# A norm's column sums: the first third laid into the last product block, and two accumulations of squares put ahead of the seventh tile's addition

## What is computed

```python
def rms_norm(x, g):
    xf = x.astype(jnp.float32)
    y = xf * lax.rsqrt(jnp.mean(xf * xf, axis=-1, keepdims=True) + EPS)
    return (y * g.astype(jnp.float32)).astype(x.dtype)

x = x + g1 * jnp.einsum('blm,md->bld', mix, w_out[l])                 # mixer's output product
x = x + g2 * swiglu(modulate(rms_norm(x, norm2_g[l]), sh2, sc2),      # feed-forward
                    w_ffn_in[l], w_ffn_out[l])
```

## Time and profile before

| | |
|---|---|
| median of 3 executions | 2637.63 us |
| the three | 2633.22, 2637.63, 2647.82 us |
| profiled execution, its own time | 2635.52 us |
| its span in the profile | 2633.7 us |
| mean granted TensorE clock | 0.959 of full |
| TensorE matmul records, busy | 13049, 94% of the span |
| VectorE, ScalarE, GpSimd busy | 51%, 30%, 33% |
| matmul records of line 673 on `n_acc` | 72 in 7 norms |

### The profile page before, as it was taken

The page is one execution under the profiler, slowest core; times in us unless marked ns, Lnnn a source line. Parts: engine busy times, 40 slices in busy tenths (PEclk is TensorE's granted clock), DMA queues, the critical chain, the costliest instruction groups (busy, mean ns, idle before and its releaser), DMA issues.

```text
span 2633.7 us, 30775 instructions
## 1 busy us (share of the span) xinstructions
PE 2481.7 (94%) x13049; PEld 2029.7 (77%) x13049; DVE 1341.3 (51%) x1704; ACT 795.0 (30%) x1083; POOL 875.5 (33%) x613
## 2 busy tenths in 40 slices
PE   7999699999999999897999999989999989999998
PEld 4889578888888888696777778878887437788886
DVE  2997865645444434877566655564642223311113
ACT  2323661311111112335631222234433333322223
POOL 2000502233333333434034554534333002444442
PEclk9998899999999999998999999989999998999999
DMA  8233103224343342221044554521103001232331
GB/s 266 91 96 97 49 1 112 81 80 128 120 136 92 116 120 64 80 90 49 1 112 144 146 172 145 177 80 51 47 17 117 11 1 48 72 104 84 100 95 58
DMA packets 309225, 240.57 MB, mean 91 GB/s; under 512 B 10692, under 2 KB 304831, under 8 KB 309087
## 3 DMA queue, kind: packets, MB, share of 16 engines
q1 hardware_dynamic: 308674, 238.47, 29.9%
q10 hardware_dynamic: 414, 0.13, 0.0%
HBM read 232.29 MB, written 2.10 MB: 89 GB/s over the span
## 4 chain that ended last, share of the span: by engine, by line
PE 87%; DVE 8%; ACT 3%; issue 1%; DMA 1%; POOL 0%; SPq 0%; DVEq 0%; ACTq 0%
PE ps L2486 61%; PE ps L1148 5%; PE ps L2521 3%; PE ps L722 2%; PE ps L935 2%; DVE mod_w L2118 1%; PE ps L1168 1%; PE ps L673 1%; DVE mod_ctx L2118 1%; PE ps L2401 1%; DVE qk_lo L875 1%; PE ps L2438 1%; PE ps L1191 1%; PE ps L749 1%; ACT probs L979 1%
## 5 line engine op out<-in xcount | busy, mean ns | idle before, releaser
L1631 POOL TENSOR_TENSOR w_lo<-raw,w_hi 128x512 fp32r<-128x512 f32 x518 | 756.5, 1490 | 1576.6 <-ACT w_hi L1732 1576.6
L2486 PE MATMUL ps<-h_hi,w_hi 128*128 128x512 f32 x1994 | 650.3, 372 | 25.1 <-DVE h_lo L2082 21.0
L2486 PE MATMUL ps<-h_lo,w_hi 128*128 128x512 f32 x1994 | 640.5, 367 | 0.0
L2486 PE MATMUL ps<-h_hi,w_lo 128*128 128x512 f32 x1994 | 639.6, 367 | 0.0
L1732 ACT ACTIVATE w_hi<-raw 128x2048 fp32r<-128x2048 f32 (+2 forms) x155 | 264.9, 1709 | 595.3 <-PE ps L2486 368.5
L2486 PEld LDWEIGHTS ps<-h_hi,w_hi 128*128 128x128 f32 x1994 | 341.0, 191 | 94.0 <-issue 23.1
L2486 PEld LDWEIGHTS ps<-h_hi,w_lo 128*128 128x128 f32 x1994 | 340.3, 190 | 66.7
L2486 PEld LDWEIGHTS ps<-h_lo,w_hi 128*128 128x128 f32 x1994 | 341.0, 191 | 65.7 <-issue 0.2
L2009 ACT ACTIVATE xg<-ps 128x512 f32<-128x512 f32 (+1 forms) x66 | 44.2, 670 | 678.5 <-PE ps L2486 491.6
L2118 DVE SCALAR_TENSOR_TENSOR mod_w<-mod_w,cond 128x512 f32<-128x512 f32 x224 | 240.7, 1075 | 3.4
L2486 PE MATMUL ps<-hid_hi,w_hi 128*128 128x512 f32 x704 | 232.1, 370 | 0.0
(11 more groups left out here) (367 smaller groups left out, 3244.5 us busy)
## 6 DMA issues: line engine op xcount, KB each, us to landing
mod_w<-in_w_mod SPq DMA_DIRECT2D x72, 1024.0 KB, 9.4
raw<-in_w_ffn_in SPq DMA_DIRECT2D x88, 512.0 KB, 5.3
raw<-in_w_in SPq DMA_DIRECT2D x54, 512.0 KB, 5.1
raw<-in_w_ffn_out SPq DMA_DIRECT2D x48, 384.0 KB, 3.8
raw<-in_w_out SPq DMA_DIRECT2D x24, 512.0 KB, 4.7
raw<-in_w_gate SPq DMA_DIRECT2D x22, 512.0 KB, 4.0
raw<-in_w_up SPq DMA_DIRECT2D x22, 512.0 KB, 5.4
raw<-in_w_down SPq DMA_DIRECT2D x24, 384.0 KB, 3.9
```

Source lines behind the costliest of these rows:

```text
L1631: ins = pool.tensor_tensor(w_lo[:, s, at:end], raw[:, s, at:end], w_hi[:, s, at:end].bitcast(F32), ALU.subtract)
L2486: ins = pe.matmul(ps[0:m, at:at + tw], weight(part, k, cols), v[:, held[k] if held else k, t0:t0 + tw], start=(at_k == 0 and j == 0 and no ...
```

## The change

On VectorE, `add_block(ni, 2)` (the accumulation of the squares of tiles 4 and 5) is issued ahead of the wait on `gemm_tile` and of tile 6's addition to `x`, instead of behind that addition. On TensorE, the column sums of `n_acc` (the first of three sources) are issued in the last block of products, for its second output tile, behind contraction step `k_tiles - 2`, so that one step of three products still follows; the norm itself then begins with the second source. Norm 0 keeps all three sources where they were. The waits stay the same: PSUM's bank half 0 free, and five accumulations done; they are now met inside the product stream.

```diff
@@ -2136,6 +2136,7 @@
                 for t in range(2):
                     if ni and b == 3 and t == 0:
+                        add_block(ni, 2)
                         dve.wait_ge(gemm_tile, ni)
                     else:
                         dve.wait_ge(gemm_done, n + 1)
@@ -2146,7 +2147,6 @@
                     if ni and b == 3 and t == 0:
                         ins.then_inc(n_x, 1)
-                        add_block(ni, 2)
@@ -2410,17 +2410,21 @@
-            def norm(ni, next_block):
-                pe.wait_ge(psum_free[0], freed(next_block)) if next_block else None
+            def norm_sum(ni, next_block, i):
+
+                if i == 0:
+                    pe.wait_ge(psum_free[0], freed(next_block)) if next_block else None
+                    pe.wait_ge(n_added, NORM_ADDED * (ni + 1))
+                else:
+                    pe.wait_ge(n_sq, KD * ni + KD - 2 + i)
+                ins = token_columns(pe, 0, (n_acc[:, :], sq[:, 0, :], sq[:, 1, :])[i], norm_tokens(ni) // P, i == 0, i == 2)
+                if i == 2:
+                    ins.then_inc(n_ss, 1)
+
+            def norm(ni, next_block, first=0):
                 T = norm_tokens(ni)
-
-                for i, (src, needed) in enumerate(((n_acc[:, :], None), (sq[:, 0, :], KD - 1), (sq[:, 1, :], KD))):
...
-                ins.then_inc(n_ss, 1)
+                for i in range(first, 3):
+                    norm_sum(ni, next_block, i)
@@ -2503,6 +2507,8 @@
                             if among and (t, at_k) != (tiles - 1, k_tiles - 1):
                                 among(t, at_k)
+                            if ni and t == 1 and at_k == k_tiles - 2:
+                                norm_sum(ni, n + 1, 0)
@@ -2554,7 +2560,7 @@
-                norm(2 * l, base_in[l])
+                norm(2 * l, base_in[l], 1 if l else 0)
@@ -2751,7 +2757,7 @@
-                norm(2 * l + 1, base_ffn[l])
+                norm(2 * l + 1, base_ffn[l], 1)
@@ -2768,7 +2774,7 @@
-                norm(6, blocks_used)
+                norm(6, blocks_used, 1)
```

More of the change, by code:

```diff
@@ L2411, in first_mods @@
                         ins.then_inc(mod_cols, 1)
-            def norm(ni, next_block):
-                pe.wait_ge(psum_free[0], freed(next_block)) if next_block else None
-                T = norm_tokens(ni)
-                for i, (src, needed) in enumerate(((n_acc[:, :], None), (sq[:, 0, :], KD - 1), (sq[:, 1, :], KD))):
[L2418 to L2422, removed]
-                ins.then_inc(n_ss, 1)
+            def norm_sum(ni, next_block, i):
[8 more added lines that the diff above has]
+            def norm(ni, next_block, first=0):
+                T = norm_tokens(ni)
+                for i in range(first, 3):
+                    norm_sum(ni, next_block, i)
                 pe.wait_ge(psum_free[1], freed(next_block)) if next_block else None
```

## The result

| | kernel before | changed kernel |
|---|---|---|
| median of 20 executions each | 2637.57 us | 2647.16 us |
| lowest to highest | 2633.22 to 2647.82 | 2635.41 to 2651.30 |
| profiled execution, its span | 2633.7 us | 2633.6 us |
| granted clock in the span | 0.959 | 0.960 |

The account below looks back on a forecast made before the run. TensorE's product stream was taken to bound the kernel (87% of the chain). Boundary terms +1.11, +1.20, 0.88, 1.0, 0.88, 0.88 gave +5.95, say 6.0 us, from 2636.6 to 2642.6; range 2633 to 2652.

Parts of the forecast that it names:

- The price of a record: In the product stream: each small sum costs 0.11 us, so 1.32 for twelve and 0.88 for eight.
- ScalarE's branch ends last at four of the six boundaries: Between last product and root: TensorE's sums end last at only two of six boundaries, once by only 0.23 us.
- sums done over 1.5 us ahead of the root: Sign at the third, fifth and sixth boundary: root still directly behind ScalarE's weights or load, sums done long before.
- No wait on `n_acc`: Second and sixth boundary: TensorE meets no stall on the fifth accumulation, with 0.2 and 0.5 us to spare.
- the 0.12 to be won back: Second boundary: tile 7's addition no longer waits for the accumulations, giving back 0.12 us; net there +1.20.
- the fourth boundary, +1.93 for +1.0: Fourth boundary: a 1.9 us stall in mid-product replaces the 1.88 behind it; root at 1753.60 against 1752.64, net +1.0.
- Then 1.32 of sums and 0.88 of products: Fourth boundary, TensorE behind the mid-product stall: sums and remaining products take these times; last product ends at 1748.77.
- the rival in which waits spread to other boundaries: Mid-product waits also at second and sixth boundary, clock falling inside: 2642.6 + 3.8 + 6 = 2652.4; chance 0.09.
- the upper bound of 0.145 for a record: Product stream: a record costs at most the fourth boundary's tail rate, 5.23 / 36; 60 records then cost 8.7 us.
- The clock's phase behind the boundaries: Products after each boundary: a small shift changes their half-clock loss between 1.5 and 3.0 us; 2638.5 to 2647.7; chance 0.20.
- The rival that the change does nothing: Whole kernel: the order only looks different, 0 us, 2636.6; chance 0.16 shared with records costing nothing.
- the sums are swallowed: Records cost nothing in the stream and the fourth boundary's stall goes: -2.6 us, 2634.0; chance 0.16, shared with no difference.

Follow-up runs that it names:

- the accumulations alone: Kernel before with only `add_block(ni, 2)` moved ahead of the wait on `gemm_tile`, the sums left behind the last product; ratio 1.0004 (0.9992 to 1.0017).
- the even boundaries only: Changed kernel with `n_acc` sums inside the last block only at the second, fourth and sixth boundary; ratio 1.0016 against the kernel before.
- the sums alone: Changed kernel with the accumulations of tiles 4 and 5 put back behind tile 6's addition; ratio 1.0055 against the kernel before, 14.5 us slower.
- the sums four times: Changed kernel with the `n_acc` sums issued three times more in the same place, into unread PSUM columns; ratio 1.0177 against the kernel before, 46.7 us.
- the changed kernel with the root first: Changed kernel with ScalarE taking the root ahead of the early weights' high parts; ratio 1.0019 against the kernel before, +5.0 us.
- the root first: Kernel before with ScalarE taking the root ahead of the early weights' high parts, sums where they were; ratio 1.0002 (0.9991 to 1.0013).
- the root first and six accumulated: Kernel before, root ahead of the early weights' high parts, tile 6's square also accumulated into `n_acc` at odd boundaries; ratio 0.9997 (0.9987 to 1.0008).

## Why the prediction was right

**What held.** The sign, the size (+6.0 forecast, +6.6 measured) and the way to it. The price of a record from layer 1's head sums, 0.11, gave 0.88 and 1.32; the third and sixth boundary came out at 0.88 and 0.90. The reading that ScalarE's branch ends last at four of the six boundaries held, and with it that nothing comes back there. The sign given for it, sums done over 1.5 us ahead of the root, did not: they were done 0.7 ahead at the third boundary and 0.2 at the sixth, and ended last at the fifth. I had taken the tail to shorten by what was moved out of it, and at the third and the sixth it shortened by nothing, because its last part waits for tile 7's square. No wait on `n_acc` appeared in the changed kernel at the second or sixth boundary: its accumulations were done at 1040.94 + 2.92 = 1043.86 at the second, 1.1 before the sums. At the second boundary the 0.12 to be won back was a misreading: tile 7's addition ended 1.21 behind the last product before, and 1.18 is what it takes when nothing holds it up, so it had lost 0.03; the accumulations alone won 0.01 there. The 2642.6 is 4.6 under the median of twenty; 1 us of that is the base (2637.6 against the 2636.6 used), 0.6 the ratio, the rest is how medians and ratio differ.

**What was mis-sized: the fourth boundary, +1.93 for +1.0.** The step is "Then 1.32 of sums and 0.88 of products", which took both at full clock. The stall itself was 1.33, not 1.9, which by itself would have made the term smaller; the sums took 1.99 and the products 1.49, 1.3 more than counted. I had that only as a piece of the rival in which waits spread to other boundaries. It needs no spreading: it happened at the one boundary where I did forecast the wait. But it need not happen either. The sums and products behind that wait were slow in the changed kernel, with the even boundaries only, with the sums alone and with the sums four times, and at the full clock in the changed kernel with the root first, where the fourth boundary took 13.39, 0.2 less than my sum gave it. And 0.63 of the excess came back behind the root, where my count did not go: to the next products the boundary cost +1.30. That the whole came so near the forecast, with this term 0.9 short at the root, is in part luck. At the fifth boundary the clock fell under the tail without any stall: tile 7's eight sums took 1.88 there and 1.05 at the third, and so came to be last, +1.04 for +0.88. And the upper bound of 0.145 for a record was too low: in the fourth boundary's stream it was 1.99 / 12 = 0.17.

**The clock's phase behind the boundaries**, the largest rival: it moved, and cancelled. The six 8 us stretches from the products' return had mean grants of 0.81, 0.62, 0.62, 0.75, 0.80 and 0.76 before; two of those after are:

```profile
469.40:477.40 8.00, 7.99 (x30) 6.86 (x31) 7.89 (x15) 3.60 (x7) 0.00 (x0) 0.63 0.47 128
1059.40:1067.40 8.00, 7.35 (x24) 5.33 (x24) 7.89 (x15) 3.53 (x7) 0.01 (x1) 0.81 0.06 16
```

The first two boundaries have traded places; the other four are at 0.61, 0.82, 0.82 and 0.61, and over all six the loss, 8 x (1 - mean) each, is 13.6 where it was 13.1. It scatters single executions and gives no sign. The Trainium skill (TensorE: Matmul & The Clock Gate, What's actually happening) calls the gate's window free-running, and the point of the switch run-variable for the same kernel. The runs agree: the fourth boundary, with the same order of its sums, took 12.62 in the kernel before, 14.34 with the root first and 12.59 with the root first and six accumulated.

**The rival that the change does nothing** is out, by the interval of the timed runs and by the run with the sums four times. **That the sums are swallowed** is out by that run too. The contention of GpSimd with VectorE's accumulations was argued from their durations (0.96 before w_lo runs, 1.43 and 1.86 beside it), and not tried by itself. The Trainium skill (GPSIMD Engine Reference, section Specifications) names such contention for VectorE instructions with two SBUF inputs, without a size; these durations agree with it.

## What to carry to other kernels

Work taken off the end of a stage is worth only what lies between it and the next branch; here that was 0.2 us at one of six places, and nothing at most others, while the same work inside a saturated product stream cost its full length every time. Before moving it, write down for each place which branch ends last and by how much, and also what the rest of the shortened branch still waits for. Price the moved instructions by neighbours of the same kind in the same kind of place. If the moved work brings a wait with it, give the clock a term of its own: behind the stand in mid-product at the fourth boundary it had fallen in four profiles out of five. And measure a boundary to where the saturated stream starts again, not to a milestone ahead of it.

## What the runs showed of the hardware that was not expected

TensorE's granted clock can fall from the 2.4 to the 1.2 GHz level while the engine is busy without a gap. It did so inside a run of 48 one-column records at the first boundary of the kernel with the sums four times (7.79 us, where 36 at full clock took 4.16), ahead of which products had run without a pause. The stretches there (TensorE's busy time behind the length, the grant third from the end):

```profile
461.00:463.00 2.00, 2.00 (x21) 2.00 (x20) 0.00 (x0) 0.00 (x0) 0.00 (x0) 1.00 0.00 0
463.00:465.00 2.00, 2.00 (x14) 2.00 (x13) 0.00 (x0) 0.00 (x0) 0.00 (x0) 0.62 0.00 0
465.00:467.00 2.00, 2.00 (x11) 2.00 (x11) 0.00 (x0) 0.00 (x0) 0.00 (x0) 0.50 0.00 0
```

It did so at the second boundary too (48 records in 7.37), and not in the run of 32 at the third (3.46). The three sources of sums behind the last product, 36 records, took 4.16, 5.19, 5.23, 5.78 or 6.92 us in different places and executions of the same code, by how early the clock fell; this spread alone is more than any of the orders tried here won at a boundary.
